# Paged latent attention in a decoder step: cache pages stored twice, by key and turned, in place of transposes on the chip

## The reference: what is computed

```python
ckv_past = cache_ckv[l][page_table].reshape(b_s, past_len, MLA_KV_LORA)
kpe_past = cache_kpe[l][page_table].reshape(b_s, past_len, MLA_ROPE_DIM)
...
for ckv, kpe, mask in key_sets:
    s = (jnp.einsum('bthc,bsc->bhts', q_lat, ckv) + jnp.einsum('bthr,bsr->bhts', q_pe, kpe)).astype(jnp.float32) * scale
...
probs = jax.nn.softmax(jnp.concatenate(scores, axis=-1), axis=-1)
...
    part = jnp.einsum('bhts,bsc->bthc', probs[..., start:stop].astype(ckv.dtype), ckv)
```

## Time and profile before

| | us |
|---|---|
| median of 3 runs | 1849.55 |
| lowest, highest | 1843.7, 1853.56 |
| the profiled execution | 1849.35 |
| its span, first to last instruction | 1847.5 |

### The profile page before, as it was taken

How to read it: one execution, slowest core, us unless ns; L and a number is a source line. 1 busy time by engine, 2 the same in 40 slices (tenths; PEclk the granted TensorE clock), 3 DMA queues, 4 the chain that set the end, 5 groups by cost and what they waited for, 6 DMA issues and landing times.

```text
span 1847.5 us, 27633 instructions
## 1 busy us (share of the span) xinstructions
PE 1769.6 (96%) x11068; PEld 1314.6 (71%) x11068; DVE 577.1 (31%) x1320; ACT 450.3 (24%) x975; POOL 112.6 (6%) x190
## 2 busy tenths in 40 slices
PE   7999899999999999999999989999999999999997
PEld 5676567777767767777766755677777677777775
DVE  1431365332022253330035214652320231633201
ACT  3233233122131231110132432321311332311100
POOL 1003000010010010000010030000100100100000
PEclk9999999999999999999999999999999999999999
DMA  8523312164337433333264133221634373333431
GB/s 314 171 85 87 148 60 104 47 238 187 114 137 295 165 120 137 137 142 118 77 227 159 41 87 148 88 76 49 284 120 155 141 302 132 113 137 137 142 114 49
DMA packets 67057, 257.83 MB, mean 140 GB/s; under 512 B 8561, under 2 KB 36658, under 8 KB 39666
## 3 DMA queue, kind: packets, MB, share of 16 engines
q1 hardware_dynamic: 55010, 200.57, 30.5%
q0 software_dynamic: 11360, 54.21, 7.8%
q10 hardware_dynamic: 560, 1.30, 0.2%
HBM read 246.85 MB, written 9.19 MB: 139 GB/s over the span
## 4 chain that ended last, share of the span: by engine, by line
PE 90%; DVE 4%; ACT 2%; issue 2%; DMA 1%; ACTq 0%; POOL 0%; DVEq 0%; POOLq 0%
PE banks L789 40%; PE banks L818 16%; PE banks L740 7%; PE banks L773 6%; PE banks L796 4%; PE banks L847 4%; PE banks L737 4%; PE banks L745 3%; PE banks L1047 1%; PE banks L1016 1%; PE banks L1445 1%; ACT work L1529 1%; PE banks L1464 1%; DMA weight_ring<-in_w 1%; DVE work L1913 1%
## 5 line engine op out<-in xcount | busy, mean ns | idle before, releaser
L789 PE MATMUL banks<-h_normed,weight_ring 128*128 128x288 f32 x1888 | 459.4, 406 | 1.1 <-ACT h_normed L1529 1.1
L789 PEld LDWEIGHTS banks<-h_normed,weight_ring 128*128 128x128 f32 x1888 | 358.6, 190 | 100.4 <-ACT h_normed L1529 1.5
L818 PE MATMUL banks<-h_normed,weight_ring 128*128 128x288 f32 x1024 | 281.6, 419 | 3.2 <-ACT values_by_token L1701 3.1
L818 PEld LDWEIGHTS banks<-h_normed,weight_ring 128*128 128x128 f32 x1024 | 189.6, 192 | 63.5 <-issue 9.3
L789 PE MATMUL banks<-work,weight_ring 128*128 128x288 f32 (+1 forms) x960 | 226.8, 399 | 1.8 <-issue 1.8
L789 PEld LDWEIGHTS banks<-work,weight_ring 128*128 128x128 f32 x960 | 182.2, 190 | 46.1 <-issue 2.6
L1529 ACT ACTIVATE work<-banks 128x512 f32<-128x512 f32 (+8 forms) x204 | 93.9, 460 | 292.8 <-PE banks L745 77.1
L773 PE MATMUL banks<-h_normed,weight_ring 128*128 128x288 f32 x480 | 124.0, 410 | 0.0
L1913 DVE TENSOR_TENSOR squares<-squares 128x288 f32<-128x288 f32 (+2 forms) x40 | 20.3, 508 | 329.4 <-ACT squares L1567 329.2
L773 PEld LDWEIGHTS banks<-h_normed,weight_ring 128*128 128x128 f32 x480 | 88.5, 190 | 31.6 <-issue 9.8
L847 PE MATMUL banks<-h_normed,weight_ring 128*128 128x288 f32 x288 | 80.8, 441 | 19.4 <-DMA weight_ring<-in_w 13.1
(11 more groups left out here) (304 smaller groups left out, 1711.7 us busy)
## 6 DMA issues: line engine op xcount, KB each, us to landing
weight_ring<-in_w SPq DMA_DIRECT2D x171, 1024.0 KB, 4.8
work<-in_mem_k POOLq DMA_DIRECT2D x12, 1024.0 KB, 11.4
work<-in_mem_v POOLq DMA_DIRECT2D x12, 1024.0 KB, 9.7
work<-in_pool SPq DMA_DIRECT2D x128, 80.0 KB, 2.0
weight_ring<-in_pool SPq DMA_DIRECT2D x64, 80.0 KB, 1.9
projected<-in_mem_k POOLq DMA_DIRECT2D x4, 1024.0 KB, 24.8
projected<-in_mem_v POOLq DMA_DIRECT2D x4, 1024.0 KB, 7.1
weight_ring<-in_pool POOLq DMA_DIRECT2D x32, 80.0 KB, 2.2
```

The source lines that it names most:

```text
L789: last = mm(ps[:, bank, 0:width], block_of(first + k), rhs(k), start=k == 0, stop=k == n - 1)
L818: last = mm(ps[:, BANK[g], 0:N], block_of(t[2] + k), H[:, k, :] if t[0] == "gate" else O[:, 2 * n + k, :], start=k == 0, stop=k == t[3] - 1)
```

## The change

The cache is packed on the host in two arrays. `pool` holds for each page its 128 latent rows of 128 numbers and, beside them, the same page turned (128 rows by number, 128 keys each): 256 numbers a row, 128 KB a page. `rotated` holds each page's rotated rows turned, 32 rows of 128, 16 KB. A batch is now 32 DMAs, and the transposes, ScalarE's copies and VectorE's packing are gone; `scores` reads the pages as loaded. The buffers are larger, so three batches have room of their own, the third only after earlier MLA work is through; batch 3 and 7 lie in the weight ring, 4, 5 and 6 where 0, 1 and 2 were. The releases of the loads and the order of TensorE's work follow that. The forget gate columns go into the tile of the input gate, which makes the layer's input stream 13 slots; a small product moves them to row 0. RWKV's last doubling step no longer computes the transpose, and the samples' two products with the incoming state are one of 8 columns.

```diff
-EACH.update({f"kv_full{b}": 16 * PAGES for b in range(NB)})
+EACH.update({f"kv_full{b}": 32 * PAGES for b in range(NB)})
...
+        own = [groups(work, 4 * GROUP * k) for k in range(3)]
+        lent = [groups(slots, 3 * SLOT * P), groups(slots, 0)]
+        kv = own + lent[:1] + own + lent[1:]
...
+        slot_after = {N_IN: 3, N_IN + 1: 3, N_IN + 2: 7, N_IN + 3: 7}
+        S_BANK = (4, 5, 0, 1)
...
-        def cache(eng, layer, b):
+        def cache(eng, layer, b, parts=range(4)):
 
             at_b = [eng.value_load(pages[0:1, b * PAGES + p:b * PAGES + p + 1], min_val=0, max_val=POOL - 1)
-                    for p in range(PAGES)]
-            for p, page in enumerate(at_b):
+                    for p in range(PAGES) if p % 4 in parts]
+            for p, page in zip([p for p in range(PAGES) if p % 4 in parts], at_b):
+                i, j = p // 4, p % 4
                 src = t_in["pool"][layer, bass.ds(page, 1)].rearrange("g p a -> (g p) a")
-                eng.dma_start(page_of(b, p), src).then_inc(S(f"kv_full{b}"), 16)
+                eng.dma_start(kv[b][j][:, i, :], src).then_inc(S(f"kv_full{b}"), 16)
+                src = t_in["rotated"][layer, bass.ds(page, 1)].rearrange("g p a -> (g p) a")
+                eng.dma_start(kr[b % 4][32 * j:32 * j + 32, i * P:(i + 1) * P], src).then_inc(S(f"kv_full{b}"), 16)
...
+                                sp.wait_ge(*before("post_ffn_done", KD))
-                        for b in {4: [0], 6: [1], 8: [2, 3]}.get(s, []):
+                        for b in {4: [0], 7: [1]}.get(s, []):
                             cache(sp, layer, b)
+                    sp.wait_ge(*at("mla_ql"))
+                    cache(sp, layer, 2, (0, 1, 2))
+                    sp.wait_ge(*at("mla_ol", 2))
+                    cache(sp, layer, 2, (3,))
                     for b in (4, 6):
-                        sp.wait_ge(*at("gemm_done", block_done(kv_after[b])))
+                        sp.wait_ge(*at("mla_pv", b - 3))
                         cache(sp, layer, b)
...
-                    pool.wait_ge(*at("gemm_done", block_done(kv_after[5])))
+                    pool.wait_ge(*at("gemm_done", block_done(SLOT * (N_IN - 3))))
+                    pool.wait_ge(*at("mla_pt", 2))
+                    cache(pool, layer, 3)
+                    pool.wait_ge(*at("mla_pv", 2))
                     cache(pool, layer, 5)
-                    pool.wait_ge(*at("mla_pv", 1))
+                    pool.wait_ge(*at("gemm_done", block_done(SLOT * (N_IN - 1))))
+                    pool.wait_ge(*at("page_scores", 4))
                     cache(pool, layer, 7)
...
+                    put(ps[0:4, 5, 0:N], C("ident", 8, 8)[:, F_AT:F_AT + 4], PR[0:8, MIX1, :]).then_inc(S("ml_f"), 1)
...
-                    def turns(b, j):
...
+                        if b == 4:
+                            pe.wait_ge(*at("mla_olc", 2))
+                        pe.wait_ge(*at(f"kv_full{b}", 32 * PAGES))
+                        mm(ps[:, bank, :], m_qpz[:, g, P * f:P * f + P], kr[b % 4], start=f == 0, stop=True, skip_group_check=True)
                         for j in range(4):
-                            last = add(ps[32 * j:32 * j + 32, g % 2, :], m_qz[:, g, 32 * f:32 * f + 32], m_kt[:, j, :])
+                            last = add(ps[32 * j:32 * j + 32, bank, :].rearrange("p (i k) -> p i k", i=4),
+                                       m_qz[:, g, 32 * f:32 * f + 32], turned(b, j))
...
+                    scores(0)
+                    scores(1)
+                    fill(4)
+                    maxima(0)
+                    scores(2)
+                    maxima_back(0)
+                    scores(3)
+                    shares(0)
+                    fill(2)
+                    values(0)
+                    fill(4)
+                    outputs(0)
+                    fill(3)
+                    maxima(1)
+                    fill(2)
+                    maxima_back(1)
+                    fill(4)
+                    shares(1)
+                    fill(2)
+                    values(1)
+                    fill(4)
+                    outputs(1)
+                    fill(1)
+                    scores(4)
+                    fill(5)
+                    scores(5)
+                    fill(2)
+                    maxima(2)
+                    fill(3)
+                    maxima_back(2)
+                    scores(6)
+                    shares(2)
+                    fill(2)
+                    values(2)
+                    fill(2)
+                    outputs(2)
+                    scores(7)
                     mix(2)
...
-                            for s in chunks_of(i):
+                            for s in () if level in RW_LAST else chunks_of(i):
                                 last = put(ps[s, bank, (4 + h) * n:(5 + h) * n], r_tt[i][s, h, 0:n], r_x[i][s, h, 0:n])
...
+                            both = ps[r, 4 + hp, TP:N + NS].rearrange("p (k b t) -> p k b t", k=2, b=NB)[:, :, b, :]
+                            last = add(both, r_s0[r, hp, b * 64:(b + 1) * 64], r_rg[r, hp, b, :, :])
...
+    a["pool"] = np.concatenate([i["cache_ckv"], i["cache_ckv"].swapaxes(2, 3)], -1)
+    a["rotated"] = np.ascontiguousarray(i["cache_kpe"].swapaxes(2, 3))
```

## The result

The changed kernel takes 1873.9 us (median of 4 runs, 1872.8 to 1874.6) against 1846.7 us for the kernel before, measured beside it (4 runs, 1843.7 to 1853.6): a ratio of 1.0142, 95% interval 1.0121 to 1.0163. It is slower by 1.4%, some 27 us. The forecast was 1868.5 us, 1846 to 1888. The profiled execution has a span of 1872.6 us. Of all executions in this document one, of the first experiment's kernel, took 2290.8 us at a mean granted clock of 0.741, and is left out of the medians and ratios.

A forecast was written before the change was run, and what follows sets the result against it. TensorE, busy 96%, bounds the kernel; after the change, page DMA issue makes it wait. Page stretches +13.9 and +11.4, RWKV -7.0, start of layer 1 +0.8: +19.1 on 1849.35 gives 1868.5 us, range 1846 to 1888.

The forecast's parts named there:

- three waits: TensorE waits per layer in the page stretch, ended by page DMAs, of about 15, 11 and 17 us.
- The loads: Page loads on SP and POOL: number loads of about 9 us, then 32 DMAs 0.56 to 0.59 us apart, per batch.
- the sum: The step-by-step reckoning of layer 0's page stretch, from own scores at 122.7 to batch 7's scores at 216.8 us, before clock.
- The rival of cheap small pieces: 16 KB pieces issue at 0.33 instead of 0.56 us, a batch is 3.7 us shorter, no change: 1847 us; chance 0.10.
- The work that left: Transposes and the forget gate's own projection tile go: 20.8 us of TensorE work leave each page stretch.
- pages-in-time rival: Pages flow by bytes and no wait replaces the removed work, deciding at about 25 us a batch: 1801 us; chance 0.14.
- The page stretch as a whole: From own scores to the eighth batch's page scores: 98.0 us, against 84.1 in layer 0 and 86.6 in layer 1.
- The clock: TensorE runs cold after waits in the page stretch: 2 x 1.7 = 3.4 us per layer, ends 0 and 7.
- The rival of a clock cold throughout: TensorE's clock stays at 1.2 GHz through the page stretch, 16 us per layer instead of 3.4: 1894 us; chance 0.06.
- Crowded engines: SP's and POOL's page streams together hold the DMA engines some 85%; fits barely, up to 1.5 us a batch otherwise.
- RWKV: Halved last doubling step and merged incoming-state products save 3.5 us per layer, taken whole: 7.0 us for both layers.
- Start of layer 1: Batch 0's loads wait for the last residual tile, so weight slot 5 lands late: 0.8 us, ends 0 and 2.

The follow-up runs named there:

- the first experiment's kernel: The changed kernel with the page numbers of batches 3, 4 and 5 loaded into registers before the queue's wait, not after; 1839.7 us, ratio to before 0.9953.

## Why the prediction was right, and where its terms were off

The forecast of slower, its mechanism and its three waits hold. That 1868.5 came within 5.4 us of the measured 1873.9 is in part luck: the forecast starts from a profiled execution 2.6 us above the median measured beside the changed kernel, and the change itself is 27 us where 19.1 were forecast. Step by step, in layer 0's time (layer 1 shifted by the 925.55 us between the two stretches' starts, 122.71 and 1048.26); the predicted times have the clock's 1.7 us added where it moves them:

| point | predicted | layer 0 | layer 1 |
|---|---|---|---|
| batch 3 landed | 145.6 | 145.9 | 146.9 |
| wait before it | 15 | 14.8 | 15.7 |
| batch 4 landed | 181.3 | 182.3 | 184.8 |
| wait before it | 11 to 12 | 12.1 | 12.8 |
| batch 6 landed | 208.1 | 209.1 | 212.0 |
| wait before it | 17 | 15.1 | 15.4 |
| batch 7 scored | 220.2 | 222.3 | 225.2 |

- **The loads.** Right. The gap ahead of a batch on SP, from the end of an issue, was predicted as 8.9 and is 9.0 us; POOL's spacing was 0.59 and is 0.59 to 0.60. SP's was taken as 0.56 and is 0.52 to 0.53, 1.0 us less over a batch. Against that, from the last issue to the scores it is 3.2 us for batch 4 (179.11 to 182.33) and 4.3 for batch 6 (204.76 to 209.10), where the sum had 2.1 for a landing. The two cancel: batch 6's scores come 26.8 us after batch 4's, as predicted. The third wait is 15 and not 17 because TensorE came to it later, 11.6 us after the start of batch 4's scores for the 9.4 of the sum; 2.1 of that is the cold clock, which the sum left to this wait without taking it off (182.33 to 189.01 for 182.78 to 187.33 with the waits filled). The gap is the number loads, as the trace shows. The rival of cheap small pieces falls: on SP a 16 KB piece is issued in the same 0.33 us with the same distance as a page, and the run without the pieces gave 25 us of waits back.
- **The work that left.** Right: 17.6 and 19.7 us less busy time in spite of the cold clock, against 20.8 counted. None of it showed in the time.
- **The pages-in-time rival** put the turn at about 25 us a batch, and that fits: 9 us less per batch turn 27 us lost into 24 won, so that by interpolation, an estimate, the kernels draw level at about 24 us. Waits of 1 to 7 us remain. What failed in that rival is only the condition, that the gap hides by itself. It doesn't; it had to be moved.
- **The page stretch as a whole.** Mis-sized, 98.0 predicted, 99.6 and 102.5 measured. In layer 0, 1.1 of the 1.6 us came behind the last wait: 13.2 us from batch 6's scores to the end against the 10.4 + 1.7 of the sum. 0.7 of it is the clock, 2.4 us for 1.7, and 0.4 the work itself up to the values, 4.0 us warm for 3.6. Layer 1 is 2.9 us longer than layer 0. Batch 3 accounts for 1.0 (24.2 us from the own scores to its scores for 23.2; its 31 intervals on POOL take 19.5 us for 18.3, with the pause of 0.89 us), the burst of TensorE's work behind it for 0.8 (6.4 for 5.6), and batches 4 and 6 for 1.1 (31.6 us from the values to batch 4's scores for 30.8, 27.2 between the two for 26.8). Bytes can explain only the last part: with half of them it is 30.5 and 26.2 us, and batch 3 is no earlier. What holds POOL up within batch 3 stays open.
- **The clock.** 1.7 us per burst was the term; 1.6 and 2.4 measured. Filling the waits shortens the stretches by 1.4 us in layer 0, whose third burst stayed cold, and by 5.3 in layer 1, against 3.4 predicted. The rival of a clock cold throughout falls: the granted clock is 0.78 over the stretch, not 0.50.
- **Crowded engines.** 85% was estimated for two queues at once and 0.85 stands in the row of 166 to 178 us. It fits, barely, as the sum had it; the cost in layer 1 is about 2 us, by the run with half the bytes.
- **RWKV.** The term that failed: 7.0 us predicted (its parts, 1.0, 0.3 and 2.1, add to 3.4 per layer and not 3.5), 3.1 (1.1 to 5.2) measured. The products went at the predicted price; the step that was wrong is "so I take it whole". Between removed products stand copies by ScalarE, of which the edit adds three, and TensorE now waits for them. Behind the two stretches the profiled executions are 4.2 and 3.1 us shorter than before, 7.3 in all, as if the term were right. The two edits by themselves don't give that. Part of the other 4 us is chance: the profiled execution of before was 2.6 us above the median, and ran from 360 to 400 us at a granted 0.91 where that of the changed kernel ran at 1.00. The rest stays open.
- **Start of layer 1.** 0.8 predicted, 0.6 measured from its first product to the end of the own scores (113.4 against 112.8), of which 0.58 is the product that was added for the forget gate (969.70 to 970.28). The late weight slot cost nothing: no product waits for it, and the token products take 14.1 us for 13.9.

By the profiled spans: +15.5 and +15.9 for the stretches, -4.2 and -3.1 behind them, +0.5 and +0.6 ahead of them, 25.2 together, against 25.1 between 1847.5 and 1872.6. Predicted were 19.1; the difference is in the stretches, 6.1 us. The medians are 27 us apart, since the profiled execution of before lay 2.6 us above the median that was measured beside the changed kernel.

## What to carry to other kernels

Count the instructions of a queue, not its bytes: a batch of pages was bound by its 32 issues and by 16 register loads ahead of them, at a DMA share under a half. Whatever a queue can do before its wait (loading addresses, here 9 us per batch) belongs before it; but move it only as far as what is late next, since the same move took 6 us off a wait behind one bound and nothing behind another. And a layout that saves TensorE's work by more transfers pays only if they still arrive in time: here it lost 27 us, and won 24 once the number loads stood ahead of the waits.

## What the runs showed of the hardware that I had not expected

- A 16 KB and a 128 KB DMA with the address in a register cost SP the same, 0.52 to 0.53 us apart; on POOL they are 0.59 to 0.60 us apart, with 0.51 and 0.56 us for the instruction.
- ScalarE's queue issued 16 small pieces in 7.95 us (0.50 each), and its elementwise work waited 8.2 us for that. No run shows what this wait cost by itself.
- A product with 8 columns cost what one with 4 cost: 1.10 us for 32 records of either.
- 39 us of additional products per layer, put into waits, delayed nothing. The mean granted clock rose from 0.966 to 0.991 by them, and the two page stretches became 1.4 and 5.3 us shorter in the profiled executions.
